# A fused two-block kernel: a second place beside the weight ring, another order from the mLSTM scores to the mixed output, and gate rows spread whole

## The reference, cut to what matters

```python
c_act = silu(c)
for i in range(2):
    mod = c_act @ ada_w[i] + ada_b[i]            # six rows of 1024
    sh1, sc1, g1, sh2, sc2, g2 = split(mod, 6)
    h = rmsnorm(x, norm_g[i, 0]) * (1 + sc1) + sh1
    y = mlstm_mixer(h, ...) if i == 0 else sgu_mixer(h, ...)
    x = x + g1 * rmsnorm(y, norm_g[i, 1])
    h = rmsnorm(x, norm_g[i, 2]) * (1 + sc2) + sh2
    x = x + g2 * rmsnorm(square(relu(h @ ffn_w1[i])) @ ffn_w2[i], norm_g[i, 3])

# inside mlstm_mixer, 2 chunks of 128 tokens (t = 0, 1), 8 heads
scores = (q @ k.T) * decay                        # per chunk and head
num = inter * (q @ c_prev) + scores @ v           # "pv"; c_prev from chunk 0 ("c_loc")
den = inter * (q @ n_prev) + sum(scores)
hh = num / max(abs(den), exp(-m));  hh = hh * rsqrt(mean(hh * hh))
y = (sigmoid(o) * hh * hnorm_g) @ w_out           # "mix_a", then "a_out"
```

## Time and profile before

| | |
|---|---|
| median of 3 runs | 1808.25 us (1805.47 to 1810.51) |
| the profiled execution's own time | 1807.92 us |
| its span in the profile | 1806.1 us |
| TensorE matmul busy | 1535.2 us, 85% of the span |
| VectorE / ScalarE / GpSimd busy | 58% / 29% / 29% |
| DMA | 486.91 MB, mean 270 GB/s |

### The profile page before, as it was taken

One profiled execution on the slowest core, in us unless ns is written; L12 is line 12 of the kernel. 1 busy time (PEld: TensorE's weight loads), 2 busy tenths in 40 slices (PEclk: granted clock), 3 DMA queues, 4 the chain that ended last, 5 costly groups with the idle time before them and its releaser, 6 DMA issues.

```text
span 1806.1 us, 20370 instructions
## 1 busy us (share of the span) xinstructions
PE 1535.2 (85%) x8119; PEld 1079.7 (60%) x8119; DVE 1052.3 (58%) x1843; ACT 516.1 (29%) x722; POOL 521.2 (29%) x575
## 2 busy tenths in 40 slices
PE   4996998999999999989998986777776778886776
PEld 4876898879787998878875873222222223422224
DVE  3365655345485655445986589565655656654443
ACT  3333443334334454334222202111111112112111
POOL 3000000001000000000000165766666666666662
PEclk8998998999999999989999988999999989999999
DMA  9568656759665555554322499999999999999993
GB/s 356 204 251 251 227 178 219 209 193 303 256 254 176 174 185 187 186 181 146 121 101 97 178 408 418 382 372 370 371 356 354 376 374 360 375 383 367 362 367 155
DMA packets 115721, 486.91 MB, mean 270 GB/s; under 512 B 13120, under 2 KB 13280, under 8 KB 99248
## 3 DMA queue, kind: packets, MB, share of 16 engines
q0 software_dynamic: 78032, 282.26, 41.4%
q1 hardware_dynamic: 37600, 203.44, 31.5%
HBM read 484.18 MB, written 1.45 MB: 269 GB/s over the span
## 4 chain that ended last, share of the span: by engine, by line
PE 52%; POOL 16%; DVE 10%; DMA 10%; issue 8%; ACT 2%; another core or an unknown queue 2%; SPq 0%; POOLq 0%; DVEq 0%; ACTq 0%
PE G L957 18%; PE G L967 18%; POOL late L546 8%; PE M L1519 4%; PE T L957 4%; POOL mod L546 4%; DMA ring<-in_wpack 2%; POOL arena L546 2%; DVE wlo L1607 2%; DMA ybuf<-in_peer_u,mod 2%; POOL ybuf L546 2%; DMA arena<-in_peer_v,mod 1%; DMA late<-in_wpack 1%; PE G L1007 1%
## 5 line engine op out<-in xcount | busy, mean ns | idle before, releaser
L1607 DVE TENSOR_TENSOR wlo<-ring,whi 128x2048 fp32r<-128x2048 f32 x120 | 275.0, 2292 | 285.4 <-ACT whi L568 285.1
L568 ACT ACTIVATE whi<-ring 128x2048 fp32r<-128x2048 f32 x120 | 229.4, 1912 | 372.5 <-PE G L967 187.7
L1519 PE MATMUL M<-late,cB 128*128 128x512 f32 x480 | 239.6, 628 | 64.8 <-DMA late<-in_peer_v,mod 49.1
L2394 DVE SCALAR_TENSOR_TENSOR late<-late,G 128x1024 f32<-128x1024 f32 x128 | 153.6, 1219 | 111.8 <-DMA late<-in_peer_u,mod 104.8
L1519 PEld LDWEIGHTS M<-late,cB 128*128 128x128 f32 x480 | 85.7, 194 | 217.7 <-DMA late<-in_peer_v,mod 128.0
L892 ACT ACTIVATE cB<-consts,mod 128x128 f32<-128x128 f32 x240 | 85.5, 395 | 446.1 <-PE M L1519 183.0
L1519 PE MATMUL M<-mod,cB 128*128 128x512 f32 x240 | 128.9, 668 | 55.4 <-DMA mod<-in_peer_v,mod 37.2
L546 POOL DMA_INDIRECT late<-in_peer_v,mod x128 | 122.0, 953 | 67.4 <-issue 42.8
L546 POOL DMA_INDIRECT late<-in_peer_u,mod x128 | 121.1, 946 | 42.0 <-issue 36.9
L1519 PEld LDWEIGHTS M<-mod,cB 128*128 128x128 f32 x240 | 45.7, 208 | 134.6 <-DMA mod<-in_peer_v,mod 74.4
L957 PE MATMUL G<-hTl,whi 128*128 128x256 f32 x760 | 108.3, 286 | 0.0
(11 more groups left out here) (398 smaller groups left out, 2467.0 us busy)
## 6 DMA issues: line engine op xcount, KB each, us to landing
ring<-in_wpack SPq DMA_DIRECT2D x188, 1024.0 KB
late<-in_wpack SPq DMA_DIRECT2D x4, 1024.0 KB, 21.2
late<-in_peer_u,mod POOLq DMA_INDIRECT x128
late<-in_peer_v,mod POOLq DMA_INDIRECT x128
mod<-gate_rows POOLq DMA_DIRECT2D x6, 256.0 KB, 10.0
xs<-in_x SPq DMA_DIRECT2D x1, 1024.0 KB, 13.3
arena<-in_wsT POOLq DMA_DIRECT2D x1, 1024.0 KB, 10.0
mod<-in_bs POOLq DMA_DIRECT2D x1, 1024.0 KB, 14.4
```

What stands on the lines that cost most here:

```text
L568: nc.scalar.activation(whi[:, q % 2, :], ring[:, raw % RING, :], ACT.Copy).then_inc(hi_done, 1)
L1519: ins = nc.tensor.matmul(M[:, nb, :], diags[:, k % DIAGS, :], rowbufs[g % GBUF][:, nb, :], start=(n == 0), stop=(n == NSEL - 1))
L1607: V.tensor_tensor(wlo[:, q % 2, :], ring[:, raw % RING, :], whi[:, q % 2, :].bitcast(F32), ALU.subtract).then_inc(raw_free[raw % RING], 1)
L2394: V.scalar_tensor_tensor(out=row, in0=row, scalar=1.0, in1=G[:, t, :, :], op0=ALU.mult, op1=ALU.mult, accum_out=dots[:, t, n:n + 1]).then_ ...
```

## The change

1. **A place beside the ring.** `side`, two halves in the part of `mod` from 3D to 5D, takes three modulation units: `ada0b` unit 1, `ada1b` unit 0, `ada1a` unit 1 (`SIDE`). SP issues their loads just before the ring half named in `SIDE_AT`, the second and third when TensorE is done with the one before (`side_free`). The squares of `y` that used this memory go to `junk0` for the first output.
2. **Named slots.** Up to the fourth half of `up0` each half has its slot written beside it (`OPENING`): while the mixer runs, the matrix halves take slots 0 and 1 and the modulation halves slots 2 and 3. Afterwards slots follow in turn.
3. **Modulation units in other places.** `ada0c`, `ada0b`, `ada0d` come earlier, `ada1b` after them; one unit of `ada1b` uses a bank of `M` in place of `G` (`SPARE_BANK`).
4. **Order from scores to mixed output** on TensorE, DVE and ACT. On DVE one low part of `a_o` and the first of `a_out` come before steps that they followed, and gate rows and picked columns move with their units.
5. **Gate rows**: one partition of each group is written (4 pieces of 512 bytes in place of 128), and the row is read back as one piece of 2 KB for each partition.

The modulation halves and matrix halves are the same, as are their sums; nothing is left out.

```diff
 FEWER = {"down0": 2, "down1": 2, "b_out": 2, "att": 2, "conv": 2,
-         "ada0c": 1, "ada0b": 1, "ada0d": 1, "ada1a": 1, "ada0e": 1, "ada1h": 0}
+         "ada0b": 1, "ada1b": 0, "ada1a": 1, "ada0e": 1, "ada1h": 0}
...
-SHARED = {("ada0c", 0): ("ada0c", 0, True), ("ada0c", 1): ("ada0b", 0, False), ("ada0b", 0): ("ada0b", 1, False),
-          ("ada0b", 1): ("ada0b", 2, True), ("ada0d", 0): ("ada0d", 0, False), ("ada0d", 1): ("ada0d", 1, True),
-          ("ada1a", 0): ("ada1a", 0, False), ("ada1a", 1): ("ada1a", 1, True), ("ada0e", 0): ("ada0e", 0, False),
-          ("ada0e", 1): ("ada0e", 1, True), ("ada1c", 0): ("ada1c", 0, False), ("ada1h", 0): ("ada1c", 1, True)}
...
+SHARED = {("ada0b", 0): ("ada0b", 0, True), ("ada0b", 1): ("ada0d", 0, False), ("ada0d", 0): ("ada0d", 1, False),
+          ("ada1b", 0): ("ada0d", 2, True), ("ada1a", 1): ("ada1a", 0, False), ("ada1a", 0): ("ada1a", 1, True),
+          ("ada0e", 0): ("ada0e", 0, False), ("ada0e", 1): ("ada0e", 1, True), ("ada1c", 0): ("ada1c", 0, False),
+          ("ada1h", 0): ("ada1c", 1, True)}
+SPARE_BANK = ("ada1b", 1)
+
+SIDE = [("ada0b", 1), ("ada1b", 0), ("ada1a", 1)]
+SIDE_AT = {("ada0c", 0): ("ada0b", 1), ("ada0d", 2): ("ada1b", 0), ("ada1b", 2): ("ada1a", 1)}
+
+OPENING = [("ada0a", 0, 0), ("ada0a", 1, 1), ("ada0a", 2, 2), ("ada0a", 3, 3),
+           ("a_qk", 0, 0), ("a_qk", 1, 1), ("a_qk", 2, 2), ("a_qk", 3, 3),
+           ("a_v", 0, 0), ("a_v", 1, 1), ("ada0c", 0, 2), ("ada0c", 1, 3), ("a_v", 2, 0),
+           ("ada0c", 2, 2), ("ada0c", 3, 3), ("a_v", 3, 1), ("a_o", 0, 0),
+           ("ada0b", 0, 2), ("ada0b", 1, 3), ("a_o", 1, 1), ("a_o", 2, 0),
+           ("ada0d", 0, 2), ("ada0d", 1, 3), ("a_o", 3, 1), ("a_out", 0, 0), ("a_out", 1, 1),
+           ("ada0d", 2, 2), ("ada0d", 3, 3), ("a_out", 2, 0), ("ada1b", 2, 2), ("ada1b", 3, 3), ("a_out", 3, 1),
+           ("up0", 0, 2), ("up0", 1, 3), ("ada1a", 0, 0), ("ada1a", 1, 1), ("up0", 2, 2), ("up0", 3, 3)]
...
+SLOT = [slot for _, _, slot in OPENING]
+for h in range(len(OPENING), len(ORDER)):
+    SLOT.append((SLOT[-1] + 1) % RING)
+USE = [SLOT[:h].count(SLOT[h]) for h in range(len(ORDER))]
+BEFORE = {(SLOT[h], USE[h]): h for h in range(len(ORDER))}
...
+        junk0 = carve(arena, 0, (D,))
+        side = carve(modf, 3 * D, (2, HALF))
...
             for h, (name, j) in enumerate(ORDER):
-                if h - RING in PAIRED:
-                    sp.wait_ge(raw_free[(h + 1) % RING], (h - 3) // RING + 1)
-                    sp.sem_inc(raw_free[h % RING], 1)
-                if name in COLUMNS and RAW[name, j - j % 2] % RING == RING - 1:
+                if (name, j) in SIDE_AT:
+                    unit, i = SIDE_AT[name, j]
+                    if (unit, i) != SIDE[0]:
+                        sp.wait_ge(sem("side_free"), SIDE.index((unit, i)))
+                    for half in range(2):
+                        sp.dma_start(side[:, half, :], slot_source(A["wpack"], unit, 2 * i + half)).then_inc(sem("side_full"), 16)
+                before = BEFORE.get((SLOT[h], USE[h] - 1))
+                if before in PAIRED:
+                    sp.wait_ge(raw_free[SLOT[before + 1]], USE[before + 1] + 1)
+                    sp.sem_inc(raw_free[SLOT[h]], 1)
...
-                pool.dma_start(row_dram[u], rbias[:, u, :]).then_inc(sem("row_out"), 16)
+                pool.dma_start(row_dram[u].rearrange("(j n) -> j n", j=4), rbias[0:P:32, u, :]).then_inc(sem("row_out"), 16)
...
-                load(part.rearrange("p (j n) -> p j n", j=4),
-                     bass.AP(row_dram.tensor, u * P * P, [[0, P], [32 * P, 4], [1, P]]), f"l_row{u}")
+                load(part, row_dram[u].partition_broadcast(P), f"l_row{u % 2}")
...
             out_gate(0)
+            split_one("a_out", 0, 0)
             head_squares(0)
-            out_gate(1)
             head_roots(0)
             head_squares(1)
             head_roots(1)
-            split_one("a_out", 0, 0)
+            out_gate(1)
             mixed_high("mix_a")
             split_one("a_out", 0, 1)
...
+                    if (name, i) == SPARE_BANK:
+                        pe.wait_ge(m_free, SPARE0["pv1"] + 1)
...
+                    elif (name, i) in SIDE:
+                        pe.wait_ge(sem("side_full"), 32 * (SIDE.index((name, i)) + 1))
+                        w, done = side, sem("side_free")
...
-            modulation_columns("ada1b", (0,))
+            modulation_columns("ada0c", (0,))
...
-            modulation_columns("ada1b", (1,))
+            modulation_columns("ada0c", (1,))
...
-            modulation_columns("ada0c", (0,))
+            modulation_columns("ada0b", (0,))
...
             score_turn(0)
-            gate_part(0, 1)
-            modulation_columns("ada0c", (1,))
...
             score_turn(1)
-            gate_part(1, 0)
+            gate_part(0, 1)
             pv(0)
-            modulation_columns("ada0b", (0,))
+            modulation_columns("ada0b", (1,))
             turned("n_loc", 1)
             spare("qc")
...
+            modulation_columns("ada0d", (0,))
+            pv(1)
+            gate_part(1, 0)
             gate_part(1, 1)
-            pv(1)
-            modulation_columns("ada0b", (1,))
-            modulation_columns("ada0d")
+            modulation_columns("ada1b", (0,))
             for g in range(4):
                 pe.wait_ge(sem("mixed_a"), g // 2 + 1)
                 turn_stream("mix_a", ybuf, (g,))
-            simple(wide, hT, "a_out", ready=mixed_split("mix_a"))
-            modulation_columns("ada1a")
+                if g == 1:
+                    modulation_columns("ada0d", (1,))
+            simple(wide, hT, "a_out", 1, ready=mixed_split("mix_a"))
+            modulation_columns("ada1b", (1,))
+            simple(wide, hT, "a_out", 1, 1)
+            modulation_columns("ada1a", (1, 0))
...
-                else:
-                    pick_columns("ada0c", 0)
...
-            bias_columns("ada1b")
+            bias_columns("ada0c")
             split_one("a_o", 0, 1)
+            gate_row("ada0b", 0)
...
-            split_one("a_o", 1, 1)
-            pick_columns("ada0c", 1)
...
-            row_sums(1)
-            bias_columns("ada0c")
-            link(V.tensor_copy(den[:, 0, :], rsum[:, 0, :]))
+            split_one("a_o", 1, 1)
             spare_done("pv0")
             spare_read(V.tensor_copy(dec[:, 0, :, :], M8), "pv0")
+            link(V.tensor_copy(den[:, 0, :], rsum[:, 0, :]))
             denominators(0)
+            gate_row("ada0b", 1)
...
+            head_means(0)
+            row_sums(1)
...
-            head_means(0)
-            gate_row("ada0b", 0)
...
             head_scaled(0)
+            split_one("a_out", 0, 0)
             head_means(1)
-            gate_row("ada0b", 1)
...
+            pick_columns("ada1b", 0)
             pick_columns("ada0d", 1)
             bias_columns("ada0d")
-            split_one("a_out", 0, 0)
             turned_in("mix_a")
             split_one("a_out", 0, 1)
             split("a_out", 1)
+            pick_columns("ada1b", 1)
+            bias_columns("ada1b")
             scale_column(0, 1)
```

More of the change, by code:

```diff
@@ L44 @@
 DIAGS = 8
-UNITS = [("ada0a", 2), ("ada0z", 2), ("a_qk", 2), ("ada1b", 2), ("a_v", 2), ("ada0c", 2), ("a_o", 2), ("ada0b", 2), ("ada0d", 2),
+UNITS = [("ada0a", 2), ("ada0z", 2), ("a_qk", 2), ("ada0c", 2), ("a_v", 2), ("ada0b", 2), ("a_o", 2), ("ada0d", 2), ("ada1b", 2),
          ("a_out", 2), ("ada1a", 2), ("up0", 8), ("ada0e", 2), ("down0", 8), ("ada1c", 1), ("ada1h", 1), ("b_u", 4), ("ada1f", 2),
@@ L106, in ring_order @@
 def ring_order():
-    order = []
+    order = [(name, j) for name, j, _ in OPENING]
     for name, n in UNITS:
@@ L113, in ring_order @@
                 order += [(later, j) for j in range(count) if (later, j) not in order]
-            order += [(name, j) for j in (2 * i, 2 * i + 1) if name != "ada0z" and (name, j) not in order]
+            if name != "ada0z" and (name, i) not in SIDE:
+                order += [(name, j) for j in (2 * i, 2 * i + 1) if (name, j) not in order]
     return order
@@ L133, in signal @@
         return "front_used", i + 1
+    if (name, i) in SIDE:
+        return "side_free", SIDE.index((name, i)) + 1
     if name == "out":
@@ L1686, in columns @@
             def columns(name):
-                for i in range(dict(UNITS)[name]):
+                for i in (1, 0) if name == "ada1a" else range(dict(UNITS)[name]):
                     pick_columns(name, i)
@@ L1861, in _ @@
             split_one("a_v", 0, 0)
-            pick_columns("ada1b", 0)
+            pick_columns("ada0c", 0)
             spare_done("cum")
@@ L1868, in _ @@
             split_one("a_v", 0, 1)
-            pick_columns("ada1b", 1)
+            pick_columns("ada0c", 1)
             split_one("a_v", 1, 0)
```

78 lines of the change are left out of this document (40 added, 38 removed).

## The result

The changed kernel takes 1791.45 us (median of 19 runs, the lowest 1784.97) against 1807.92 (19 runs, 1801.93 to 1818.06) for the kernel before: ratio 0.991, 95% interval 0.9897 to 0.9923, which is 13.9 to 18.6 us faster. (One run of 7767.59 us is left out of the ratio.) Forecast were 1794.4, a gain of 13.8 on the profiled execution, and a range of 1789 to 1802: the time is in the range, and the measured gain lies a little above the forecast one.

A forecast was written before the change was run, and what follows sets the result against it. The ring was taken to hold back `a_out`, with the mixer's own chain behind it. The norm 15.8 us earlier less 2.0 for the clock gave 13.8: 1794.1 from 1807.92, median 0.3 higher, 1794.4; range 1789 to 1802.

The forecast's parts named there:

- What bounds it: Before `a_out`: the ring alone held it back by more than ten microseconds, with the mixer's own chain behind.
- Up to the head scores: From `a_v` to the end of the first head scores: 117.92 becomes 116.2, 1.7 us gained.
- Scores to `a_out`: From head scores through mixed output: last transposes end and `a_out` begins at 154.2 against 169.85, 15.7 us earlier.
- four before use: `ada0d` halves 2 and 3: issued at 137.4, there at 145, four microseconds before TensorE uses them.
- Gate rows: Rows at about 110 and 134: even at the old price each has four microseconds to spare, so 0.
- the bound of 4.9: Gate rows: at most 4.9 us lost in one landing, against nothing gained.
- `a_out` and after it: `a_out` takes 23.7 us, then 7.4 to the norm with a table load; the norm starts 15.8 us earlier.
- Clock: TensorE's waits before `a_out` and before the norm: 1 us lost at each, 2 in all, bounds nothing and 7.
- A: Rival on ScalarE: each added table switch takes 2.56 us, twice the row; 1.8 us lost, 1796.2; chance 0.12.
- B: Rival: half clock through the first half of `a_out`, or one exposed landing; 5 us more, 1799.4; chance 0.15.
- D: Rival: SP's waits in series leave six landings open at 4.93 each, 29.6 us; slower, 1824; chance 0.06.
- C: Rival: no gain, moved gate quarters hold the mixed output and `a_out` waits as before; 1808; chance 0.07.

The follow-up runs named there:

- new rows alone: The kernel before with only the gate rows written and read as after the change: 1806.77 us against 1810.34, ratio 0.9981.
- the table experiment: The changed kernel with a one-column square root after the second output gate, loading the root's table there and not after `a_out`: 1792.2 us, one run.
- plain slots: The changed kernel with every half in the slot of its number modulo four in place of named slots: 1802.96 us, one run.
- the doubled unit: The changed kernel with the 64 matmuls of the last `ada1a` unit done twice, same result: 1790.0 us, one run.
- the earlier `ada0e`: The changed kernel with one half of `down0` loaded ahead of `ada0e` in place of two: 1794.05 us, ratio 0.993 to the kernel before.
- all three edits: The changed kernel with early root table, last `ada1a` unit done twice, and `ada0e` loaded earlier with `down0`'s second half split late: 1783.07 us, ratio 0.9868.

## Why the prediction was right

**What bounds it: right in the main.** The long wait for the ring held `a_out` back; with it gone 13.72 us are won up to the full mark, against 13.8 forecast. But the ring was not alone in it: with the old order and all else new the full mark is at 131.13, so 5.6 of the 13.7 are won without the order and the rest needs both.

**Up to the head scores: right.** Forecast 1.7, measured 44.10 - 42.42 = 1.68; the wait for the low part is 1.24 in place of 2.40. By the profile with new rows alone, 46.15, it would be 3.7: the agreement to a tenth owes something to the one profile that the forecast was read from.

**Scores to `a_out`: right.** The walk put the first group of `mix_a` 32.0 us behind the end of the head scores (116.2 to 148.2). The scores take 1.16 from their mark, so it is 75.61 - 42.42 - 1.16 = 32.03. Then it allowed 6.0 to `a_out`, and there are 6.16. But "four before use" for the halves of `ada0d` was too generous. By the landing records they are issued at 135.72 and 136.09, as forecast (137.4 on the clock of the profile before, 1.72 later), but take 7.0 and 9.8 us, not 4.93 and 2.5 more; the second lands at 145.85 and is used at 147.57, a slack of 1.7. The price was that of a lone landing, and side halves and a gate row were on their way at the same time.

**Gate rows: the step that failed.** "Even at the old price each falls beside halves with four microseconds to spare, so I take 0" does not hold; at the old price the half lands 4.16 later, so that the slack of 1.7 is overrun by 2.51, and the full mark is 4.77 later, all but the whole of the bound of 4.9 that the prediction set. The sum came out because it was walked for the rows at no cost, which is what the new rows have. The reason was wrong and the term of the sum came right by luck: without this part the change would have won 9 us.

**`a_out` and after it: right.** 24.08 against 23.7; 7.56 against 7.4, with the table load in it as forecast. Small errors add up: the norm comes 128.37 - 113.41 = 14.96 earlier in place of 15.8.

**Clock: one term of two.** Forecast 1 at the mixed transposes and 1 at the norm. At the first the clock stays at 1.00 between 140 and 160 us, at no cost; at the second 1.23. So the clock cost 0.8 less than forecast and the norm gained 0.8 less, and that the full mark is met to 0.1 is partly luck.

**Rivals.** A (longer switch) is refuted by the table experiment. B and D did not occur in this kernel, but both mechanisms are real: without the side place three waits for late halves, with the clock behind them, cost 23 us and the kernel is slower than before, and plain slots cost 8. C is excluded by the interval.

**The remainder.** In the profiled execution 1.72 us of the gain lie before `a_v`, where TensorE's work is the same in both kernels. Over the 14 profiles `a_v` begins at 70.7 to 71.1 seven times and at 72.2 to 72.8 seven times. The rows show that it is the clock. The second unit from `late`, 64 matmuls, in the kernel before and in the changed one:

```profile
29.75 3.19 PE L1007 MATMUL G<-late,cB 128*32 128x128 f32 x64 [2.94 <-DMA late<-in_wpack]
```
```profile
29.73 1.95 PE L1041 MATMUL G<-late,cB 128*32 128x128 f32 x64 [2.91 <-DMA late<-in_wpack]
```

In the seven profiles with the late start this unit takes 2.93 to 3.58 us. In the seven others it takes 1.95 or 1.96 five times, and in the two where it takes 2.58 and 2.67 the `a_qk` products behind 56 us run at full clock, which in the twelve others they partly do not. After nearly the same wait the same unit runs at either clock. With the root's table `a_v` begins at 72.42 and with the doubled unit added to it at 71.05, though neither edit touches anything ahead of it; the changed kernel had the lower value twice. Whether a program tends to one of the two stays open. With these 1.72 the two profiles differ by 15.4 at the full mark, and by 15.65 in the whole, and the medians by 16.5 where 13.5 was forecast.

**The parts are not a sum.** Taken away one at a time they cost 23.2 (side place), 8.3 (slots), 8.1 (order) and 4.8 (rows), 44 us together, for a change that wins 13.7; alone, the rows win 1.3 by the full mark (3.3 where they act). Each part is worth most when the others have taken the slack away.

## What to carry to other kernels

A wait that disappears can be worth nothing until the queue behind it is reordered too: the earlier `ada0e` won nothing until the half that it displaced was also moved behind the work that did not need it, and then it won 5.7 us. Cost a part by the slack that is left once all parts are in, not by the slack of the kernel before. And a wait ahead of TensorE can cost more than its length: here 1.7 us in the unit of 64 matmuls behind it, when that ran at half clock.

## What the runs showed of the hardware

- The same 256 KB row was read back in 11.7 us in pieces of 512 bytes and in 6.9 in pieces of 2 KB, beside ring loads both times. Over all six rows of an execution it took 8.0 to 11.7 us with old rows and 4.7 to 8.1 in the changed kernel, and in the 12 us around that pair all DMA together moved 254 and 362 GB/s. The Trainium skill, "DMA: Bandwidth & Descriptors", section "Specifications", gives 512 bytes as enough for line rate; for this row, spread to 128 partitions beside other traffic, the runs show a further gain beyond it. The edit also shrank the write of the row from 128 pieces of 512 bytes to 4 (5.8 and 5.5 us to landing); the two halves of the edit were not run apart.
- After idle times of 3.68 to 11.26 us TensorE's next work ran, in every row from `a_v` to `down0` in these profiles, at least for a part at the lower level of its clock, 1.2 GHz (64 matmuls 3.64 against 1.95, 32 transposes 5.54). After 2.81 it did not, in three kernels, nor after 2.40 in the kernel before; after 2.11 (3.62 for 64 matmuls there), 2.30, 2.42, 2.51 and 2.85 it did, wholly or in part, and after 2.40 too in the kernel with all three edits (2.58). So the length of the wait alone does not tell it.
